# The down products' first chunk: fourteen tile fetches from GpSimd's queue

## What is computed

```python
D_MODEL = 2048
D_FF = 4 * D_MODEL
...
x = layer_norm(ALPHA * x + h @ w_out, ln1_g, ln1_b)
u = jax.nn.relu(x @ w_up)
return layer_norm(ALPHA * x + (u * u) @ w_down, ln2_g, ln2_b)
```

## Time and profile before

| | us |
|---|---|
| median of 3 runs | 2784.7 |
| lowest and highest | 2781.75, 2792.43 |
| the profiled execution, its own time | 2774.81 |
| span of the profiled execution | 2773.1 |

### The profile page before, as it was taken

The page is one execution under the profiler, slowest core; times in us unless marked ns, Lnnn a source line. Parts: engine busy times, 40 slices in busy tenths (PEclk is TensorE's granted clock), DMA queues, the critical chain, the costliest instruction groups (busy, mean ns, idle before and its releaser), DMA issues.

```text
span 2773.1 us, 58914 instructions
## 1 busy us (share of the span) xinstructions
PE 2686.1 (97%) x25059; PEld 2546.8 (92%) x25059; DVE 1931.1 (70%) x2366; ACT 1094.9 (39%) x1615; POOL 339.3 (12%) x357
## 2 busy tenths in 40 slices
PE   8999999999999898899999999999998999999998
PEld 8998988888899667799989999999998999999997
DVE  3374554554554386787987787788777888888887
ACT  3221221222221375445535555555553333333331
POOL 3011101111010131111102222222220000000000
PEclk9999999999999999999999999999999999999999
DMA  7889999999999862377536666666678757565732
GB/s 241 295 315 403 413 407 412 405 409 406 411 405 373 301 201 98 104 211 203 149 118 204 189 202 180 199 192 193 188 235 278 242 180 239 161 218 173 235 98 95
DMA packets 542216, 691.84 MB, mean 249 GB/s; under 512 B 25723, under 2 KB 467164, under 8 KB 531538
## 3 DMA queue, kind: packets, MB, share of 16 engines
q1 hardware_dynamic: 465042, 477.59, 52.2%
q0 software_dynamic: 13872, 141.28, 12.5%
q10 hardware_dynamic: 63040, 69.21, 7.3%
HBM read 589.21 MB, written 98.79 MB: 248 GB/s over the span
## 4 chain that ended last, share of the span: by engine, by line
PE 47%; DVE 1%; DMA 1%; SPq 1%; issue 0%; ACT 0%; DVEq 0%; ACTq 0%
PE big_G L2390 15%; PE big_G L2392 15%; PE big_G L2391 15%; DMA raw<-in_w_down 1%; PE big_G L2499 1%; SPq L2245 0%; DMA raw<-in_w_up 0%; PE big_G L2495 0%; PE big_G L2497 0%; PE big_G L2496 0%; DVE raw L2679 0%; DVE wl L2667 0%; DVE base L2679 0%; SPq L2261 0%; DVE big_xl L2687 0%
## 5 line engine op out<-in xcount | busy, mean ns | idle before, releaser
L472 PE MATMUL prj_G<-prj_xh,prj_wh 128*128 128x280 f32 (+1 forms) x1696 | 500.5, 295 | 1.7 <-issue 1.7
L474 PE MATMUL prj_G<-prj_xh,prj_wl 128*128 128x280 f32 (+1 forms) x1696 | 495.2, 292 | 0.0
L473 PE MATMUL prj_G<-prj_xl,prj_wh 128*128 128x280 f32 (+1 forms) x1696 | 494.2, 291 | 0.0
L727 DVE STREAM_TRANSPOSE prj_kT<-base 128x4096 f32<-128x4096 f32 x64 | 284.4, 4444 | 259.3 <-PE prj_S L505 259.3
L2528 ACT ACTIVATE wh<-raw 128x768 fp32r<-128x768 f32 (+1 forms) x294 | 279.6, 951 | 373.0 <-PE big_G L2392 199.4
L2667 DVE TENSOR_TENSOR wl<-raw,wh 128x768 fp32r<-128x768 f32 (+1 forms) x294 | 329.6, 1124 | 119.8 <-ACT wh L2528 119.6
L472 PEld LDWEIGHTS prj_G<-prj_xh,prj_wh 128*128 128x128 f32 x1696 | 321.3, 189 | 25.9 <-issue 24.4
L2390 PE MATMUL big_G<-big_xh,wh 128*128 128x272 f32 x1168 | 338.7, 290 | 3.4 <-ACT base L2531 1.7
L2392 PE MATMUL big_G<-big_xh,wl 128*128 128x272 f32 x1168 | 338.2, 290 | 0.0
L2391 PE MATMUL big_G<-big_xl,wh 128*128 128x272 f32 x1168 | 336.5, 288 | 0.0
L2390 PE MATMUL big_G<-ff_window,wh 128*128 128x272 f32 x1116 | 322.6, 289 | 7.1 <-DVE wl L2667 7.1
(11 more groups left out here) (484 smaller groups left out, 6035.2 us busy)
## 6 DMA issues: line engine op xcount, KB each, us to landing
prj_v_nat<-in_cache_v SPq DMA_DIRECT2D x242, 512.0 KB, 8.1
raw<-in_w_up SPq DMA_DIRECT2D x128, 512.0 KB, 4.4
u_scratch<-base SPq DMA_DIRECT2D x60, 952.0 KB, 6.6
ff_window<-u_scratch SPq DMA_DIRECT2D x70, 816.0 KB, 7.3
prj_raw<-in_w_in ACTq DMA_DIRECT2D x103, 512.0 KB, 17.8
raw<-in_w_down SPq DMA_DIRECT2D x120, 384.0 KB, 4.7
raw<-in_w_out SPq DMA_DIRECT2D x60, 512.0 KB, 4.9
ff_left_over<-in_w_down SPq DMA_DIRECT2D x80, 192.0 KB, 6.4
```

The lines of the kernel that those rows point to most:

```text
L472: mm(out, w_hi[:, k, m], xh[:, k0 + k, cols], start=(first and k == 0), stop=False)
L473: mm(out, w_hi[:, k, m], xl[:, k0 + k, cols], start=False, stop=False)
L474: last = mm(out, w_lo[:, k, m], xh[:, k0 + k, cols], start=False, stop=(end and k == nk - 1))
L727: V.transpose(flat(kT[:, :, :, :, :].rearrange("p r h b i -> p r (h b i)")), flat(k_nat[k % 2][:, :, :]))\
```

## The change

The fourteen fills of the first chunk are issued by GpSimd in place of SP. `fill_window` moves out of SP's block and takes the engine as an argument; `fill_first` moves to GpSimd's block, where it stands ahead of the sums of the last block (b = 30); it waits for the same products of group 29 as SP did. SP's list at the border keeps weights and refills alone, with the waits that they had. The fills of the first chunk count on seven semaphores of their own (`win_first`), and TensorE waits for those at group 30; for later chunks, still fetched by SP, the counts of `win_in` are one chunk lower.

```diff
+        win_first = [sem(f"win_first{i}") for i in range(COMBOS)]
...
+        def fill_window(eng, chunk, n, j):
+
+            at = 2 * COMBOS * chunk + 2 * n + j
+            eng.dma_start(window[:, at % NSLOTS, :, :].bitcast(F32), dram["u_scratch"][chunk, j, PLACE[n]])\
+                .then_inc(win_in[n] if chunk else win_first[n], 16)
...
-            def fill_first(product, places):
-
-                sp.wait_ge(up_done, product_at(g, product))
-                for at in places:
-                    fill_window(0, at // 2, at % 2)
-
-            for i in range(2):
-                sp.wait_ge(spilled[i], 32 * (CH // 2))
-            fill_first(0, (0, 1))
             sp.wait_ge(sum_done, sums_of(g) + 4)
             load_role(g + 1, 3)
-            fill_first(1, (2, 3))
-            sp.wait_ge(lo_done, base_of(g) + 5)
-            load_role(g + 1, 0)
-            fill_first(1, (4,))
-            fill_first(2, (5,))
-            sp.wait_ge(lo_done, base_of(g) + 6)
-            load_role(g + 1, 2)
-            fill_first(2, (6, 7))
+            for role, n in ((0, 4), (2, 5)):
+                sp.wait_ge(lo_done, base_of(g) + n + 1)
+                load_role(g + 1, role)
             sp.wait_ge(y_out, 16)
             sp.wait_ge(spilled[0], 16 * NUP)
             refill_y(0)
             sp.wait_ge(lo_done, base_of(g) + 7)
             load_role(g + 1, 1)
-            fill_first(3, (8, 9))
-            fill_first(4, (10, 11))
-            fill_first(4, (12,))
-            fill_first(5, (13,))
             sp.wait_ge(up_done, product_at(g, 6))
             load_role(g + 2, 0)
...
-                            pe.wait_ge(win_in[n], 32 * (chunk + 1))
+                            pe.wait_ge(*((win_in[n], 32 * chunk) if chunk else (win_first[n], 32)))
...
+            def fill_first():
+
+                for i in range(2):
+                    po.wait_ge(spilled[i], 32 * (CH // 2))
+                for product, places in enumerate(((0, 1), (2, 3, 4), (5, 6, 7), (8, 9), (10, 11, 12), (13,))):
+                    po.wait_ge(up_done, product_at(NUP - 1, product))
+                    for at in places:
+                        fill_window(po, 0, at // 2, at % 2)
+
             for b in range(1, NUP + 1):
+                if b == NUP:
+                    fill_first()
                 po.wait_ge(relu_done, b + 1)
```

More of the change, by code:

```diff
@@ L2256, in spill @@
                                  split[i][j].rearrange("p (c t) -> p c t", c=COMBOS)).then_inc(spilled[i], 16)
[L2258 to L2262, removed]
             def refill_y(p):
@@ L2335, in _ @@
                     for j in range(2):
-                        fill_window(chunk + 1, early, j)
+                        fill_window(sp, chunk + 1, early, j)
                 sp.wait_ge(sum_done, sums_of(g) + 4)
@@ L2342, in _ @@
                         for j in range(2):
-                            fill_window(chunk + 1, n, j)
+                            fill_window(sp, chunk + 1, n, j)
                 elif more and 3 <= p < 3 + early:
@@ L2349, in _ @@
                     for j in range(2):
-                        fill_window(chunk + 1, p - 3, j)
+                        fill_window(sp, chunk + 1, p - 3, j)
                 if v == 0:
```

## The result

| | median us | runs from to | profiled execution us | its span us |
|---|---|---|---|---|
| before, timed beside the changed kernel | 2786.28 | 2779.87 to 2792.67 | 2774.81 | 2773.1 |
| changed kernel | 2793.81 | 2789.11 to 2802.30 | 2793.59 | 2791.9 |

The ratio of after to before is 1.0024, 95% interval 1.0014 to 1.0034: +6.7 us, +3.9 to +9.5. That is slower, and by less than 0.5%. It is not the quotient of the two medians in the table, which differ by 7.5 us.

The account below looks back on a forecast made before the run. TensorE, busy 97%, was taken to bound the kernel, so time follows the start of group 31's second product. +10.4 us for its delay and +1.1 for the clock, on 2784.7, gave 2796 us, range 2782 to 2806.

Parts of the forecast that it names:

- the turns: DMA engines take one packet of each queue in turn, so 0.03 us weight packets wait for 0.25 us fill packets.
- Both ways of counting: Role 0's landing at group 30: ten more fills ahead give 2100.5 us, 96 turns give 2098; 2099 was taken.
- The rival of longer turns: DMA engines take up to two weight packets for each fill packet; +8 us, 2793 us; chance 0.13.
- weights get through: SP's queue gets four or more packets per fill packet; 0.5 us earlier than before, 2784 us; chance 0.13.
- The path behind the landing: Group 30's product 1 starts 7.25 us after role 0's landing, through ScalarE's copies and VectorE's chain, at 2106.25 us.
- Step (1), SP relieved: Fourteen issues leave SP's queue: role 1's load some 5 us earlier, group 31's three loads some 8 us earlier.
- Step (2), the issue: GpSimd issues the fourteen fills as group 29's products end, 0.96 us per 512 KB issue, the last near 2078.5 us.
- Step (3), the sums: GpSimd's block 30 sums, behind the last fill, end at 2084.1 us; costed at nothing, 2.7 us if ScalarE's cover goes.
- SP's queue without the 7 us stalls: Sign named for the forecast being right: SP no longer has the 7 us stalls for fills.
- Step (6), the clock: TensorE, idle for 18 us, then works at half clock, mostly in product 0; 0 to 3.3 us, taken as 1.1.
- The cold rival: TensorE's lower clock outlasts the pause by the whole group, adding 13.5 us to the 10.4; about 2808 us; chance 0.11.
- The sum: Whole kernel: +10.4 for group 31's later product 1 plus 1.1 for the clock, +11.5 us, bounds +7 and +14.

Follow-up runs that it names:

- the run with packets of 4,352 B: Changed kernel with the spilled operand laid out so fills on GpSimd's queue read rows of 1,088 B; ratio 1.0048 (1.0032 to 1.0064).
- the run on ScalarE's queue: Changed kernel with the fourteen fills issued on ScalarE's hardware queue in place of GpSimd's; ratio 1.0015 (1.0000 to 1.0030).
- the last run with small rows: Kernel with the fourteen fills on ScalarE's queue, edited so that fills read rows of 1,088 B; ratio 1.0074 (1.0057 to 1.0091).
- the run with six: Against the kernel before, only the last six fills moved to GpSimd's queue, the first eight left on SP's; ratio 1.0034 (1.0016 to 1.0051).

## Why the prediction was right, and where it was not

**The forecast's mechanism held: the turns, and role 0's landing.** Forecast 2099 us, measured 2107.12 us, which is 2098.9 us on the scale of before. Both ways of counting (ten fills put ahead: 2100.5; 96 turns: 2098) were close, and the turns are what the counts show. The one uncertain choice, that the ratio in the earlier trace rows would hold between these two queues too, was right; it had been read from other transfers, and two hardware queues share in the same way. The rival of longer turns falls with the counts 639 to 637, and so does "weights get through". The Trainium skill, "DMA: Bandwidth & Descriptors", section "Queues, rings and completion order", has an engine switch between queues at packets, which is what the traces show; its typical 9 to 17 descriptors in a packet they don't show, since a packet here was one row (6,528, 1,088 or 512 B) or, on GpSimd's queue at 1,088 B, four.

**The path behind the landing.** 7.25 us forecast from landing to product 1, 7.14 measured (2107.12 to 2114.26 us). Roles 2 and 1 and the refill were to be in by 2103.5 us; on that scale they were in at 2101.2, 2104.0 and 2102.7, role 1 half a microsecond late. Role 1 was the nearest to binding: ScalarE waited 1.90 us for it, TensorE didn't. Group 31's loads were to be in by 2108 and were, the last at 2116.09 us, 2107.8.

**Step (1), SP relieved, was wrong.** I took SP's stalls for a matter of its own issues: fourteen fewer, so role 1's load 5 us and group 31's loads 8 us sooner. But the prediction itself had read long issues as a full queue, and SP's queue, with one small packet a turn, emptied more slowly than before. The stall went from the fills to role 2's load (5.66 us) and the refill of y (12.85 us). No view shows how full a queue is; that the issues wait for room is read from these lengths, against 0.37 us for the two loads ahead of them. Role 1's load left 10.3 us later against the end of group 29 than before, and group 31's first load 14.2 us after it where it had been 8.1. It cost nothing, because the engines, not the issues, set the landings, and the landings above were reckoned from the engines: role 1 landed 1.34 us after the refill ahead of it, no more than a load takes by itself. "SP's queue without the 7 us stalls", which I had named as a mark of being right, didn't come, and the sum stood without it.

**Step (2), the issue, was mis-sized without effect.** 0.96 us from GpSimd's stores of 512 KB; the fills' issues took 0.52 us. **Step (3), the sums,** ended by 2090.5 us, 2082.2 on before's scale (forecast 2084.1), 17 us ahead of their use; the run with the sums moved forward shows that they cost nothing.

**Step (6), the clock, was mis-sized: 1.1 us forecast, nothing paid.** The pause was 19.46 us, where the step had 18. The lower level, granted clock 0.50, lasted from 2092.20 to 2112.70 us. All 16 matmuls in it belong to product 0, which had VectorE's chain to wait for anyway; full clock was back 1.56 us before product 1 began. The cold rival falls here. A slow product 1 was not far off, though: in the run with packets of 4,352 B TensorE paused twice, and product 1 too ran at half clock.

```profile
2104.30:2120.00 15.70, 10.28 (x44) 9.97 (x45) 9.10 (x11) 3.20 (x5) 0.00 (x0) 0.50 0.94 289
```

**The sum.** +11.5 forecast, +10.4 in the trace: 1.1 of the difference is the clock. Timed it is +6.7, at most +9.5. So the trace shows more than the runs, and that stays open. The same stands at the run on ScalarE's queue (+10.9 in the trace, at most +8.4 timed), and the other way about at the last run with small rows (+10.9 and at least +15.9); in the other six the trace's number lies inside the timed interval. The traces are one execution each, and the code ahead of the change moves by up to 18 us from one to the next, so a few us between the two measures can't be placed. That code ahead is where the traces differ: in all but the last run with small rows 21.4 us lie between the spill and the end of group 29, and in all ten 50.4 to 50.9 us between the last matmul of the down products and the end of the span. The profiled execution of before, 2774.81 us, is also 5 us under the fastest of its 20 timed runs. The median forecast of 2796 us is 2.2 us above the 2793.8 measured, and that is in part luck: before came out 1.6 us slower than in the runs that the forecast was added to, and the change itself, +6.7 timed, is 4.8 us less than forecast.

**What was not seen.** That six fills would do as much as fourteen. The prediction priced the loss by counting fills ahead of role 0; the run with six shows that whatever is last on the slow queue pays for any big packets that are still there.

## What to carry to other kernels

Before moving a transfer to another queue, look at what the DMA engines do there: if they are full, a second queue saves no transfer time, it changes the order, from first come first served to one packet each in turn. Then compare the packets' sizes, because the queue with the small packets gets the small part: 512 B against 6,528 B left the weights 11% of the engines' time. Keep both on one queue and write the order down, or hold the large packets back until the transfer that the critical engine waits for is in: the run with nine fills held won 7 of the 10 us back in the trace that way. Giving that transfer the larger packets follows from the turns too, but no run here tried it.

## What the runs showed of the hardware that I had not expected

GpSimd's queue put four rows of 1,088 B into one packet of 4,352 B (0.195 us), where SP's and ScalarE's queues made a packet of each row (0.05 us). So the same access pattern takes turns of different length by who issues it.

Small rows cost the fills little by themselves: with rows of 1,088 B on one queue the engines moved 2.84 MB in 8 us, 355 GB/s (2084 to 2092 us), against 395 GB/s from 2094 to 2104 us in before. The kernel took 3.4 us longer in the trace; the +2.8 us timed (-0.8 to +6.7) can't be told from nothing.

The Trainium skill says in "DMA: Bandwidth & Descriptors", section "Issuing engines are not separate DMA queues", that issuing from several engines at once saves only issue time. The bytes agree (404 GB/s in after from 2094 to 2104 us, 395 before); the order does not stay the same, and here it cost 10.4 us in the trace.
